# Feed-forward of the first block: inner columns from X times the norm's weights, three side by side, scaled by the tokens' inverse roots on the way out of PSUM

## The chip, the cores and the metric

The kernel runs on one NeuronCore of a Trainium2 chip. TensorE (PE) multiplies, its weight loads (PEld) run beside its matmuls; VectorE (DVE), ScalarE (ACT) and GpSimd (POOL) do the elementwise work, SyncE (SP) starts the weight transfers. Each engine works through its own instructions strictly in the order in which they were written, and waits on semaphores that the others raise. The metric is the device time of one execution in microseconds (us), lower is better: the kernel before has a median of 4513.54 us over three runs (4511.9 to 4514.31).

## The reference

Two blocks follow each other, each with two layers. The change is in the first block only, in both of its layers. Of a layer this matters (S = 512 tokens, D = 1024, FFN = 2816):

```python
def rmsnorm(x, g):
    y = x * rsqrt(mean(x * x, axis=-1) + NORM_EPS)
    return y * g

x = x + rmsnorm(mixed @ w_out, norm_mix_post)
h = rmsnorm(x, norm_ffn_pre)
u = causal_dwconv(h @ w_up, conv_w, conv_b)     # three taps along the tokens, per channel
ua, ub = split(u, (FFN_DIM, FFN_DIM))
x = x + rmsnorm((gelu(ua) * ub) @ w_down, norm_ffn_post)
```

The inverse root of a token is one number for the token's whole row of `h`. It can be multiplied in before the product with `w_up` or behind it. The convolution mixes neighbouring tokens, so it has to come after the multiplication.

## The kernel before, in words

Activations are kept transposed: 128 channels on the partitions, the 512 tokens along the row. X is eight such tiles (DT = 8). A product's output is made in columns: one column is 128 output channels x 512 tokens in one PSUM bank, and takes 8 steps (one per input tile q). Each step is three matmuls (`column_step`, L350, L351, L353), since both operands are split into an upper and a lower part: upper weights x upper input, upper weights x lower input, lower weights x upper input.

Weights come in pieces of 8 tiles (512 KB), one per column here, into a ring of four slots. SP starts the transfers in the order of a fixed list, and waits before each until its slot is free (`weights`, L334). A "cut" piece is split in two: ACT writes the upper part (`act_cuts`, L297, `whi`), DVE then the lower part (`dve_cuts`, L307, `wlo`). There are two buffers of each, so ACT can cut piece k only when PE has done with piece k-2. A "raw" piece goes to PE uncut; its slot is free when PE has used it. In the feed-forward stage the list is: two cut pieces (two columns of `w_up`), two raw pieces, two cut, two raw, and so on, 22 times. The raw pieces are for sums that the second block needs (`modulation_sums`, L1913); PE makes them behind each odd column (`pe_tick`). In this text the cut pieces of the stage are numbered 0, 1, 2, ...; column n uses piece n.

`dense` writes the order of each engine: for each column first the cuts that come due, then the column's own work (the `_tick` functions). Ahead of the columns stands `first_norms`: it makes the sum of squares of the last product Z (`stat_sum`, `stat_root`, `stat_inverse`, `stat_spread`: PE, ACT, DVE, PE), adds the normed Z to X tile by tile (`add_normed`: DVE L518 and L521 for even tiles, POOL L529 for odd ones), then makes the squares of X (ACT L369), their sum, root, inverse and spread again, and only then `norm_to`: h (DVE L475), its upper part (ACT L451), its lower part (DVE L461). Columns 0 and 1 are made interleaved, as the tiles of h come (`two_columns`). In the stage, ACT copies each column out of PSUM into a buffer `u` (L1990), DVE does the three taps (L2003, L2006, L2009), ACT the gelu (L1993), POOL the product of the two halves (L2022), ACT and DVE the upper and lower part of that (L1964, L1968).

Of the kernel before, what the change touches and what calls it, by code (L numbers as in the profile page):

```python
# [7 lines left out]
F32 = mybir.dt.float32  # L8
# [6 lines left out]
P = 128  # L15
D = 1024
DT = D // P
# [83 lines left out]
LAG, PLACES = 4, 8  # L101
GP = 4
# [46 lines left out]
class Prog:  # L149
# [410 lines left out]
    def dense(self, cols, xh, xl, segs, banks_of, free, ready=None, pe_tick=None, act_tick=None,  # L560
              dve_tick=None, pool_tick=None, paired=False, hold=None):
# [4 lines left out]
        def pe():  # L566
            for n, steps in enumerate(cols):
                if paired and n == 0:
                    self.two_columns(cols, xh, xl, segs, banks_of, ready)
                elif not (paired and n == 1):  # L570
                    free(n)
                    self.column(steps, xh, xl, segs, banks_of(n), ready if n == 0 else None)
# [14 lines left out]
        def dve():  # L587
            self.dve_cuts(min(first + 1, self.ahead(first)))
            for n, steps in enumerate(cols):
                for st in steps:  # L590
                    if st.at + st.n == PIECE:
                        self.dve_cuts(self.ahead(st.cut) if hold is None else min(hold, self.ahead(st.cut)))
                if dve_tick:
                    dve_tick(n, steps[-1].value)
# [9 lines left out]
    def columns(self, n_out, kt, paired=False):  # L604

        steps = self.plan(n_out * kt)
        cols = [steps[n * kt:(n + 1) * kt] for n in range(n_out)]
        if paired:
# [10 lines left out]
    def hybrid_sems(self):  # L619
# [26 lines left out]
        self.s_emb = sem("embedded")  # L646

    def hybrid(self, layer, added):
# [49 lines left out]
        b_lo = self.recurrence_out(layer)  # L698
        return self.layer_embedding(layer, *self.conv_ffn(layer, b_lo))
# [1185 lines left out]
    def first_norms(self, Z, b_z, st, cut):  # L1885

        V, A, G = self.V, self.A, self.G
        V.wait_ge(self.s_z.h, b_z + DT)
        G.wait_ge(self.s_ld_x.h, self.s_ld_x.n)
        V.wait_ge(self.s_ld_x.h, self.s_ld_x.n)  # L1890
# [3 lines left out]
        self.x_added(V, b_add, DT - 1)  # L1894
        return self.norm_to(self.view("h", 6144, DT, S), SEG1, lambda j, si: self.p1("fpre", j), (4, 5, 6, 7),
                            Stats(self, A1 + 24000, S, 6), h_hi, h_lo, ready=lambda j: self.x_added(A, b_add, j))
# [40 lines left out]
    def conv_ffn(self, layer, b_lo):  # L1937
# [9 lines left out]
        ub = [self.view(f"u{i}", TF + i * 520, 520) for i in range(4)]  # L1947
        cv = [self.view(f"cv{i}", TF + 2080 + i * S, S) for i in range(4)]
# [9 lines left out]
        cols = self.columns(2 * FT, DT, True)  # L1958
# [21 lines left out]
        def act_tick(n, value):  # L1980
# [16 lines left out]
        def dve_tick(n, value):  # L1997
            q, h = divmod(n, 2)
            i, at = 2 * (q % 2) + h, q + FT * h
            V.wait_ge(self.s_u.h, b_u + n + 1)  # L2000
# [1203 lines left out]
def layout(i):  # L3204
    f = {n: np.asarray(v) for n, v in i.items()}
    ws = []
    for l in range(L):
# [10 lines left out]
        up, down = _inter(f["w_up"][l][:, :FFN], f["w_up"][l][:, FFN:]), _tiles(f["w_down"][l])  # L3218
        ada = _blocks(f["ada_w_2"][l])
# [92 lines left out]
```

## Time and profile before

| what | value |
|---|---|
| median of 3 runs | 4513.54 us (4511.9 to 4514.31) |
| the profiled execution | 4518.9 us, of which the span of the instructions is 4517.4 us |
| PE busy | 4186.4 us (93%) |
| PEld busy | 3242.8 us (72%) |
| DVE busy | 1965.6 us (44%) |
| ACT busy | 1514.9 us (34%) |
| POOL busy | 570.3 us (13%) |
| first norms and feed-forward of layer 0 | from about 867 us to about 1180 us for the inner columns |
| the same of layer 1 | starts at about 2219 us |
| granted TensorE clock, mean | 0.969 of full speed |

A row of the chain of waits says when a link began, how long it held the end, and which engine and line it was. A row of the timeline says start, duration, engine, line, output <- inputs, and in brackets how long the engine was idle before, and what ended that. A duration on DVE or ACT overlaps the next instruction's start a little, so the distance between two starts is what an instruction costs in a row of them.

### The profile page before, as it was taken

To read this page: it belongs to the slowest core of one execution; us is meant where nothing else is said; L and a number is where in the kernel's file an instruction comes from. 1 tells how busy PE (TensorE), PEld (TensorE's weight loads), DVE (VectorE), ACT (ScalarE), POOL (GpSimd) and SP (SyncE) were. 2 spreads that over 40 slices of the span, in tenths; PEclk is the share of its full clock that TensorE was granted. 3 is DMA by queue.
4 is the path that set the end of the run, shared out by engine and by line. 5 is a ranking of instruction groups with operands and counts; after the bars stand their busy time and mean duration, and the time that the engine had idled before them with its cause. 6 is when DMAs were issued, how large, how long until landed. Compare 5 with 4: busy or idle time off the path is not lost.

```text
span 4517.4 us, 73554 instructions
## 1 busy us (share of the span) xinstructions
PE 4186.4 (93%) x32028; PEld 3242.8 (72%) x32028; DVE 1965.6 (44%) x2957; ACT 1514.9 (34%) x2699; POOL 570.3 (13%) x402
## 2 busy tenths in 40 slices
PE   7999779899997999779899998988899999989999
PEld 5776676677775776776677776755688888667877
DVE  5536434455335536434455334357332231444232
ACT  3533233333333533223333333247221121343221
POOL 1215100011002215100011001012000000150000
PEclk9999999999998999999999998999999999999999
DMA  4132002244323132003244321100111211101222
GB/s 160 38 103 69 33 4 94 70 172 173 141 88 104 39 106 70 31 4 104 80 172 171 136 84 43 52 29 1 36 58 61 66 61 61 56 6 62 97 92 87
DMA packets 97681, 351.69 MB, mean 78 GB/s; under 512 B 10064, under 2 KB 13648, under 8 KB 95952
## 3 DMA queue, kind: packets, MB, share of 16 engines
q1 hardware_dynamic: 86480, 313.02, 20.2%
q10 hardware_dynamic: 10880, 33.96, 2.0%
q8 instruction: 254, 4.16, 0.4%
q14 instruction: 67, 0.55, 0.0%
HBM read 332.26 MB, written 14.68 MB: 77 GB/s over the span
## 4 chain that ended last, share of the span: by engine, by line
PE 82%; DVE 8%; issue 3%; POOL 3%; ACT 3%; ACTq 0%; DMA 0%; DVEq 0%; POOLq 0%; SPq 0%
PE ps L350 20%; PE ps L351 19%; PE ps L353 19%; PE ps L1368 7%; PE ps L2395 1%; PE ps L1913 1%; DVE sml L2470 1%; PE ps L391 1%; POOL e L2929 1%; PE ps L2842 1%; DVE x L521 1%; POOL dd L1218 1%; POOL ops L1234 1%; PE ps L888 1%; POOL ops L1226 1%
## 5 line engine op out<-in xcount | busy, mean ns | idle before, releaser
L307 DVE TENSOR_TENSOR wlo<-ring,whi 128x1024 fp32r<-128x1024 f32 x494 | 623.7, 1263 | 1828.6 <-ACT whi L297 1828.2
L297 ACT CAST whi<-ring 128x1024 fp32r<-128x1024 f32 x494 | 517.4, 1048 | 2094.4 <-PE ps L353 1822.6
L350 PE MATMUL ps<-h_hi,whi 128*128 128x512 f32 x1424 | 595.8, 418 | 17.7 <-DVE h_lo L461 10.2
L351 PE MATMUL ps<-h_lo,whi 128*128 128x512 f32 x1424 | 570.7, 401 | 0.0
L353 PE MATMUL ps<-h_hi,wlo 128*128 128x512 f32 x1424 | 569.9, 400 | 0.0
L350 PE MATMUL ps<-hm_hi,whi 128*128 128x512 f32 (+1 forms) x1408 | 514.3, 365 | 16.0 <-DVE hm_lo L464 14.4
L351 PE MATMUL ps<-hm_lo,whi 128*128 128x512 f32 (+1 forms) x1408 | 480.7, 357 | 0.0
L353 PE MATMUL ps<-hm_hi,wlo 128*128 128x512 f32 (+1 forms) x1408 | 418.9, 355 | 0.0
L350 PEld LDWEIGHTS ps<-h_hi,whi 128*128 128x128 f32 x1424 | 273.7, 192 | 160.3 <-issue 62.2
L350 PE MATMUL ps<-ac_hi,whi 128*128 128x512 f32 x880 | 330.3, 375 | 3.0 <-DVE wlo L307 3.0
L350 PEld LDWEIGHTS ps<-hm_hi,whi 128*128 128x128 f32 x1408 | 267.1, 190 | 86.0 <-DVE hm_lo L464 19.6
L351 PEld LDWEIGHTS ps<-h_lo,whi 128*128 128x128 f32 x1424 | 273.7, 192 | 66.5 <-issue 8.2
L353 PEld LDWEIGHTS ps<-h_hi,wlo 128*128 128x128 f32 x1424 | 273.5, 192 | 65.4
L351 PE MATMUL ps<-ac_lo,whi 128*128 128x512 f32 x880 | 318.9, 371 | 0.0
L351 PEld LDWEIGHTS ps<-hm_lo,whi 128*128 128x128 f32 x1408 | 267.1, 190 | 47.2 <-issue 4.8
L353 PE MATMUL ps<-ac_hi,wlo 128*128 128x512 f32 x880 | 297.4, 370 | 0.0
L353 PEld LDWEIGHTS ps<-hm_hi,wlo 128*128 128x128 f32 x1408 | 229.7, 189 | 19.2
L350 PEld LDWEIGHTS ps<-ac_hi,whi 128*128 128x128 f32 x880 | 165.5, 188 | 48.5 <-issue 11.7
L351 PEld LDWEIGHTS ps<-ac_lo,whi 128*128 128x128 f32 x880 | 165.7, 188 | 30.8
L353 PEld LDWEIGHTS ps<-ac_hi,wlo 128*128 128x128 f32 x880 | 152.3, 188 | 23.7
L1368 PE MATMUL ps<-zz 64*64 64x64 f32 (+1 forms) x2560 | 123.2, 239 | 10.8 <-ACT zz L1547 4.0
L2022 POOL TENSOR_TENSOR ac<-cv,cv 128x512 f32<-128x512 f32 x44 | 68.9, 1567 | 503.8 <-DVE cv L2009 503.8
(387 smaller groups left out, 7214.5 us busy)
## 6 DMA issues: line engine op xcount, KB each, us to landing
ring<-in_w SPq DMA_DIRECT2D x590, 512.0 KB, 3.3
h_spill<-h ACTq DMA_DIRECT2D x2, 2048.0 KB, 6.7
x_spill<-x ACTq DMA_DIRECT2D x2, 2048.0 KB, 14.7
m_spill<-m ACTq DMA_DIRECT2D x2, 2048.0 KB, 9.9
h_again<-h_spill ACTq DMA_DIRECT2D x2, 2048.0 KB, 9.0
ma<-m_spill ACTq DMA_DIRECT2D x2, 2048.0 KB, 10.2
x<-x_spill ACTq DMA_DIRECT2D x2, 2048.0 KB, 9.8
x<-in_x SPq DMA_DIRECT2D x4, 512.0 KB, 7.6
```

The source lines that it names most:

```text
L297: self.A.copy(self.hi[k % 2][:], raw).then_inc(self.s_cut_hi.h, 1)
L307: self.V.tensor_tensor(self.lo[k % 2][:], raw, self.hi[k % 2][:].bitcast(F32), ALU.subtract).then_inc(self.s_cut_lo.h, 1)
L350: T.matmul(ps[:, b, 0:cw], hi, xh(q, c0, cw), start=q == 0, stop=False, skip_group_check=True)
L351: T.matmul(ps[:, b, 0:cw], hi, xl(q, c0, cw), start=False, stop=False, skip_group_check=True)
L353: m = T.matmul(ps[:, b, 0:cw], lo, xh(q, c0, cw), start=False, stop=last, skip_group_check=True)
L391: m = T.matmul(self.ps[32 * g:32 * g + 32, st.bank, 0:w], self.c("ones_d", 32), st.sq[j % 2][:, g * w:(g + 1) * w], start=j == 0, stop=j = ...
L521: V.tensor_tensor(self.X[:, j, 0:S], self.X[:, j, 0:S], Z[:, j, :], ALU.add).then_inc(self.s_xadv.h, 1)
L888: T.matmul(ps[:, 7, :], hi, hh(q, 0, S), start=q == 0, stop=False, skip_group_check=True)
L1218: G.tensor_tensor(dd[n % 2][:], zb[n % 2][:, 0:S], zb[n % 2][:, 1:S + 1], ALU.subtract).then_inc(self.s_dd.h, 1)
L1226: self.gq(G.tensor_tensor(BB[:, j, :], kn[i][:], BB[:, j, :], ALU.mult))
L1368: i = T.matmul(ps[dst, 4 * g + bank, at + j * wide:at + (j + 1) * wide], lt(src, GP * g + j), rh(src, GP * g + j), start=begin and j == 0 ...
L2022: G.tensor_tensor(AC[:, q, :], cv[i][:], cv[i - 1][:], ALU.mult).then_inc(self.s_glu.h, 1)
```

## The change

`first_norms` now makes the upper and lower part of X times the norm's weights `fpre` right behind each added tile of X, with no inverse root in it. All adds are on DVE, none on POOL. `columns` and `dense` take `side=3`: columns 0, 1 and 2 are made side by side, 9 matmuls for each tile of the input, and behind each tile the sum of its squares. The weights of those three columns are laid out so that a piece holds them in that order. The inverse roots are spread into PSUM bank 3 in the middle of column 3, copied to SBUF once (`root`), and each column is then taken out of PSUM by a DVE multiplication with `root` in place of the ACT copy. For that the DVE tick stands ahead of the DVE cuts (`tick_first`). The cuts of pieces 2, 3 and 4 are now written inside `first_norms`.

```diff
+    def side_columns(self, cols, xh, xl, segs, banks_of, ready, beside):
+        for q in range(len(cols[0])):
+            ready(q)
+            for c, steps in enumerate(cols):
+                self.column_step(steps, q, xh, xl, segs, banks_of(c))
+            beside(q)
...
     def first_norms(self, Z, b_z, st, cut):
-        b_add = self.add_normed(Z, lambda j: self.p1("post", j), st, [DT - 1], (2, 3, 4, 5), cut=cut)
...
-        return self.norm_to(self.view("h", 6144, DT, S), SEG1, lambda j, si: self.p1("fpre", j), (4, 5, 6, 7),
-                            Stats(self, A1 + 24000, S, 6), h_hi, h_lo, ready=lambda j: self.x_added(A, b_add, j))
+        late = {4: first + 2, 7: first + 3}
...
+            for j in range(DT):
+                A.wait_ge(self.s_xadv.h, b_add + j + 1)
+                A.activation(h_hi[:, j, :], self.X[:, j, 0:S], ACT.Identity,
+                             scale=self.p1("fpre", j)).then_inc(self.s_nhi.h, 1)
+                self.stat_square(st2, j, self.X[:, j, 0:S])
+                if j in late:
+                    self.act_cuts(late[j])
+            self.stat_root(st2)
+            self.act_cuts(first + 4)
...
+        def lower(j):
+            V.wait_ge(self.s_nhi.h, b_hi + j + 1)
+            V.scalar_tensor_tensor(h_lo[:, j, :], self.X[:, j, 0:S], self.p1("fpre", j), h_hi[:, j, :].bitcast(F32),
+                                   ALU.mult, ALU.subtract).then_inc(self.s_nlo.h, 1)
...
+            for j in range(DT):
+                z = self.by_bank(banks, Z[:, j, :])
+                V.scalar_tensor_tensor(z, z, self.p1("post", j), self.spread_of(banks, 0, S), ALU.mult,
+                                       ALU.mult).then_inc(self.s_zn.h, 1)
+                if j >= 1:
+                    lower(j - 1)
+                V.wait_ge(self.s_zn.h, b_zn + j + 1)
+                V.tensor_tensor(self.X[:, j, 0:S], self.X[:, j, 0:S], Z[:, j, :], ALU.add).then_inc(self.s_xadv.h, 1)
+                if j in late:
+                    self.dve_cuts(late[j])
+            lower(DT - 1)
+            self.stat_inverse(st2)
+            self.dve_cuts(first + 4)
...
         def act_tick(n, value):
...
             if n == 0:
-                A.wait_ge(self.s_vq.h, zeroed)
-            A.wait_ge(self.s_mm.h, value)
-            if q >= 2:
-                A.wait_ge(self.s_conv.h, b_conv + n - 3)
-            A.copy(ub[i][:, 2:S + 2], ps[:, n % 4, :]).then_inc(self.s_u.h, 1)
+                A.wait_ge(self.s_rsq.h, st2.spread + 1)
+                A.copy(root[:], ps[:, 3, :]).then_inc(self.s_rootc.h, 1)
...
         def dve_tick(n, value):
+            if n == 0:
+                V.wait_ge(self.s_vq.h, zeroed)
+                V.wait_ge(self.s_rootc.h, b_root + 1)
+            V.wait_ge(self.s_mm.h, value)
+            if q >= 2:
+                V.wait_ge(self.s_conv.h, b_conv + n - 3)
+            V.tensor_tensor(ub[i][:, 2:S + 2], ps[:, bank(n), :], root[:], ALU.mult).then_inc(self.s_u.h, 1)
+            if h == 1 and 0 <= q - 3 < early:
+                lower(q - 3)
```

Three places show how the instructions move. Each row is the line in its own kernel, the operation and its operands, and in brackets the semaphores that it waits for.

First DVE, from the add of the normed Z on. Before, `z` is Z, `x` is X, and the rows end where h begins:

```order
L307 TENSOR_TENSOR wlo0<-ring,whi0 128x1024 [waits cut_hi]
L518 SCALAR_TENSOR_TENSOR z_8290<-z_8290,par,ps 128x512 [waits rsq]
L518 SCALAR_TENSOR_TENSOR z_8290<-z_8290,par,ps 128x512
L521 TENSOR_TENSOR x_49<-x_49,z_8290 128x512 [waits z_normed]
L518 SCALAR_TENSOR_TENSOR z_8290<-z_8290,par,ps 128x512 x2
L521 TENSOR_TENSOR x_49<-x_49,z_8290 128x512 [waits z_normed]
```

The same place on DVE in the changed kernel, at the fifth and sixth tile (`h3_lo` is the lower part of the columns' input, `wlo1` here is piece 2):

```order
L1945 SCALAR_TENSOR_TENSOR z_8290<-z_8290,par,ps 128x512
L1934 SCALAR_TENSOR_TENSOR h3_lo_9446<-x_49,par,h3_hi_9445 128x512 [waits n_hi]
L1950 TENSOR_TENSOR x_49<-x_49,z_8290 128x512 [waits z_normed]
L308 TENSOR_TENSOR wlo1<-ring,whi1 128x1024 [waits cut_hi]
L1945 SCALAR_TENSOR_TENSOR z_8290<-z_8290,par,ps 128x512
L1934 SCALAR_TENSOR_TENSOR h3_lo_9446<-x_49,par,h3_hi_9445 128x512 [waits n_hi]
```

Each tile now has three DVE instructions instead of the two and a half of adding and norming apart, and the cut of piece 2 stands in the middle of them; the cut of piece 3 stands in the same way behind the last add and ahead of the last lower part.

Second ACT, from the root of X's squares to the first gelu. Before (`inv` is the root, `h3_hi` the upper part of h, `whi1` and `whi0` are pieces 2 and 3):

```order
L378 ACTIVATE inv<-ps,con 128x128 [waits sq_mm]
L451 CAST h3_hi_9492<-h_95 128x512 [waits normed] x8
L1955 DMA pe_in_9622<-in_p 128x1024
L297 CAST whi1<-ring 128x1024 [waits mm,w_full3]
L1990 COPY u0_9614<-ps 128x512 [waits mm,dve_seq]
L297 CAST whi0<-ring 128x1024 [waits mm,w_full0]
L1990 COPY u1_9615<-ps 128x512 [waits mm]
L1993 ACT_TABLE_LOAD
L1993 ACTIVATE cv0_9618<-cv0_9618 128x512 [waits conv]
```

The same place on ACT in the changed kernel (`whi0` is piece 3, `whi1` piece 4, `h3_inv` is `root`, the last `whi0` piece 5):

```order
L378 ACTIVATE n_sq34240_512_1_9448<-x_49 128x512 [waits sq_mm]
L298 CAST whi0<-ring 128x1024 [waits mm,w_full0]
L387 ACTIVATE inv<-ps,con 128x128 [waits sq_mm]
L298 CAST whi1<-ring 128x1024 [waits mm,w_full3]
L2018 DMA pe_in_9574<-in_p 128x1024
L2051 COPY h3_inv_9569<-ps 128x512 [waits rsq]
L2054 ACT_TABLE_LOAD
L2054 ACTIVATE cv0_9570<-cv0_9570 128x512 [waits conv]
L298 CAST whi0<-ring 128x1024 [waits mm,w_full0]
```

The copies to `u` are gone, and the copy of the inverse roots stands behind the cut of piece 4, which waits for that piece's transfer (`w_full3`).

Third DVE, at the first columns. Before (`wlo0`, `wlo1`, `wlo0` are pieces 3, 4 and 5):

```order
L307 TENSOR_TENSOR wlo0<-ring,whi0 128x1024 [waits cut_hi]
L2003 TENSOR_SCALAR cv1_9619<-u1_9615,par 128x512 [waits u_copied]
L2006 SCALAR_TENSOR_TENSOR cv1_9619<-u1_9615,par,cv1_9619 128x512 [waits dve_seq]
L2009 SCALAR_TENSOR_TENSOR cv1_9619<-u1_9615,par,cv1_9619 128x512 [waits dve_seq]
L307 TENSOR_TENSOR wlo1<-ring,whi1 128x1024 [waits cut_hi]
L2003 TENSOR_SCALAR cv2_9620<-u2_9616,par 128x512 [waits u_copied]
L2006 SCALAR_TENSOR_TENSOR cv2_9620<-u2_9616,par,cv2_9620 128x512 [waits dve_seq]
L2009 SCALAR_TENSOR_TENSOR cv2_9620<-u2_9616,par,cv2_9620 128x512 [waits dve_seq]
L307 TENSOR_TENSOR wlo0<-ring,whi0 128x1024 [waits cut_hi]
```

The same place on DVE in the changed kernel. Ahead of these rows stand the cut of piece 4, column 0's four instructions and column 1's `u`; the last row is the cut of piece 5:

```order
L2073 TENSOR_SCALAR cv1_9571<-u1_9566,par 128x512 [waits u_copied]
L2076 SCALAR_TENSOR_TENSOR cv1_9571<-u1_9566,par,cv1_9571 128x512 [waits dve_seq]
L2079 SCALAR_TENSOR_TENSOR cv1_9571<-u1_9566,par,cv1_9571 128x512 [waits dve_seq]
L2067 TENSOR_TENSOR u2_9567<-ps,h3_inv_9569 128x512 [waits mm]
L2073 TENSOR_SCALAR cv2_9572<-u2_9567,par 128x512 [waits u_copied]
L2076 SCALAR_TENSOR_TENSOR cv2_9572<-u2_9567,par,cv2_9572 128x512 [waits dve_seq]
L2079 SCALAR_TENSOR_TENSOR cv2_9572<-u2_9567,par,cv2_9572 128x512 [waits dve_seq]
L2067 TENSOR_TENSOR u3_9568<-ps,h3_inv_9569 128x512 [waits mm]
L2073 TENSOR_SCALAR cv3_9573<-u3_9568,par 128x512 [waits u_copied]
L2076 SCALAR_TENSOR_TENSOR cv3_9573<-u3_9568,par,cv3_9573 128x512 [waits dve_seq]
L2079 SCALAR_TENSOR_TENSOR cv3_9573<-u3_9568,par,cv3_9573 128x512 [waits dve_seq]
L308 TENSOR_TENSOR wlo0<-ring,whi0 128x1024 [waits cut_hi]
```

Between the cuts of pieces 4 and 5 DVE had one column's three instructions before; now it has four columns' sixteen.

## Rows read from the trace of the kernel before

**Rows 1.** The page's part 4: the chain that ended last, by engine.

```profile
PE 82%; DVE 8%; issue 3%; POOL 3%; ACT 3%; ACTq 0%; DMA 0%; DVEq 0%; POOLq 0%; SPq 0%
```

**Rows 2.** The chain of waits in layer 0's first norms: start, us, engine, line.

```profile
869.67 1.11 DVE wlo L307
870.77 1.33 DVE z L518 x2
872.12 1.26 DVE x L521
...
881.78 1.22 PE ps L391 x16
...
886.81 0.70 DVE h_lo L461
887.55 0.79 PE ps L350
888.35 0.43 PE ps L351
```

**Rows 3.** Busy time by stretch, layer 0: PE, PEld, DVE, ACT, POOL, granted clock, DMA.

```profile
872.00:873.00 1.00, 0.00 (x0) 0.00 (x0) 0.97 (x2) 0.00 (x0) 0.84 (x1) 0.76 0.74 299
...
893.00:894.00 1.00, 1.00 (x6) 0.83 (x5) 1.00 (x3) 0.62 (x1) 0.00 (x0) 1.00 0.00 0
```

**Rows 4.** Timeline of POOL, the first odd tile's add.

```profile
871.58 1.26 POOL L529 TENSOR_TENSOR x<-x,z 128x512 f32<-128x512 f32 x1 [102.43 <-DVE z L518]
```

**Rows 5.** DVE's column multiplication out of PSUM, by tile `gb`: ns min/median/max.

```profile
L1854 DVE TENSOR_TENSOR gb<-ps,gb x16: 682/684/685, 780.9 to 2172.7; 128x512 f32<-128x512 f32 x16
```

**Rows 6.** Timeline of ACT: two squares of X, one upper part of h.

```profile
873.42 1.15 ACT L369 ACTIVATE n_sq<-x 128x512 f32<-128x512 f32 x2 [3.90 <-DVE x L521]
...
888.19 0.62 ACT L451 CAST h_hi<-h 128x512 fp32r<-128x512 f32 x1 [0.76 <-DVE h L475]
```

**Rows 7.** Timeline of PE: a sum of squares between matmuls, then raw pieces, then columns.

```profile
860.50 0.39 PE L353 MATMUL ps<-mix_hi,wlo 128*128 128x512 f32 x1
...
861.18 0.50 PE L350 MATMUL ps<-mix_hi,whi 128*128 128x512 f32 x1
...
901.30 1.06 PE L1913 MATMUL ps<-ring,cond 128*32 128x512 f32 x8
902.45 0.51 PE L350 MATMUL ps<-h_hi,whi 128*128 128x512 f32 x1
...
926.97 0.50 PE L350 MATMUL ps<-h_hi,whi 128*128 128x512 f32 x1
```

**Rows 8.** Timeline of DVE: one column's taps between two cuts.

```profile
902.32 0.54 DVE L2003 TENSOR_SCALAR cv<-u,par 128x512 f32<-128x512 f32 x1
902.89 0.75 DVE L2006 SCALAR_TENSOR_TENSOR cv<-u,par,cv 128x512 f32<-128x512 f32 x1
903.68 0.75 DVE L2009 SCALAR_TENSOR_TENSOR cv<-u,par,cv 128x512 f32<-128x512 f32 x1
904.35 1.22 DVE L307 TENSOR_TENSOR wlo<-ring,whi 128x1024 fp32r<-128x1024 f32 x1
905.49 0.54 DVE L2003 TENSOR_SCALAR cv<-u,par 128x512 f32<-128x512 f32 x1
```

**Rows 9.** Timeline of ACT: cuts that waited for a transfer, layer 0.

```profile
909.36 1.05 ACT L297 CAST whi<-ring 128x1024 fp32r<-128x1024 f32 x1 [4.26 <-DMA ring<-in_w]
...
921.08 1.05 ACT L297 CAST whi<-ring 128x1024 fp32r<-128x1024 f32 x1 [5.13 <-DMA ring<-in_w]
```

**Rows 10.** Timeline of SP's queue: the fourth transfer behind the first raw pieces.

```profile
905.59 0.33 SPq L334 DMA_DIRECT2D ring<-in_w  x1
```

**Rows 11.** Timeline of PE in the second block: a column behind a short gap.

```profile
4400.74 0.47 PE L350 MATMUL ps<-ac_hi,whi 128*128 128x512 f32 x1 [2.12 <-DVE wlo L307]
```

**Rows 12.** Busy time by stretch behind that gap, columns as in rows 3.

```profile
4402.00:4405.00 3.00, 3.00 (x8) 2.30 (x7) 0.00 (x0) 0.00 (x0) 0.00 (x0) 0.50 0.83 274
```

More of the change, by code:

```diff
@@ L560, in dense @@
     def dense(self, cols, xh, xl, segs, banks_of, free, ready=None, pe_tick=None, act_tick=None,
-              dve_tick=None, pool_tick=None, paired=False, hold=None):
+              dve_tick=None, pool_tick=None, paired=False, hold=None, side=0, beside=None, between=None,
+              tick_first=False):
         first = cols[0][0].cut
@@ L569, in pe @@
                     self.two_columns(cols, xh, xl, segs, banks_of, ready)
-                elif not (paired and n == 1):
+                elif side and n == 0:
+                    self.side_columns(cols[:side], xh, xl, segs, banks_of, ready, beside)
+                elif not (paired and n == 1) and n >= side:
                     free(n)
-                    self.column(steps, xh, xl, segs, banks_of(n), ready if n == 0 else None)
+                    self.column(steps, xh, xl, segs, banks_of(n), ready if n == 0 else between(n) if between else None)
                 if pe_tick:
@@ L589, in dve @@
             for n, steps in enumerate(cols):
+                if tick_first:
+                    dve_tick(n, steps[-1].value)
                 for st in steps:
@@ L592, in dve @@
                         self.dve_cuts(self.ahead(st.cut) if hold is None else min(hold, self.ahead(st.cut)))
-                if dve_tick:
+                if dve_tick and not tick_first:
                     dve_tick(n, steps[-1].value)
@@ L602, in dense, with columns @@
         return pe(), act(), dve(), pool()
-    def columns(self, n_out, kt, paired=False):
+    def columns(self, n_out, kt, paired=False, side=0):
         steps = self.plan(n_out * kt)
         cols = [steps[n * kt:(n + 1) * kt] for n in range(n_out)]
+        for c in range(side):
+            cols[c] = steps[c:side * kt:side]
         if paired:
@@ L1895, in first_norms @@
-        return self.norm_to(self.view("h", 6144, DT, S), SEG1, lambda j, si: self.p1("fpre", j), (4, 5, 6, 7),
-                            Stats(self, A1 + 24000, S, 6), h_hi, h_lo, ready=lambda j: self.x_added(A, b_add, j))
+        st2 = Stats(self, A1 + 24000, S, 6)
+        b_zn, b_add = self.s_zn.take(DT), self.s_xadv.take(DT)
+        b_hi, b_lo = self.s_nhi.take(DT), self.s_nlo.take(DT)
+        cols, banks = self.columns(2 * FT, DT, side=SIDE), (2, 3, 4, 5)
+        first = cols[0][0].cut
@@ new lines, in first_norms, with pe, act @@
+        late = {4: first + 2, 7: first + 3}
+        def pe():
+            self.stat_sum(st, DT - 1)
+            self.stat_spread(st, banks)
+            yield
+        def act():
+            self.stat_root(st)
+            self.act_cuts(cut)
+            for j in range(DT):
[7 more added lines that the diff above has]
+            self.act_cuts(first + 4)
+            yield
@@ L1935, in modulation_sums, with conv_ffn @@
         return pe, pe_back, act, dve
[L1937 removed]
+    def conv_ffn(self, layer, cols, b_lo, st2):
         T, V, A, G, ps = self.T, self.V, self.A, self.G, self.ps
@@ L1947, in conv_ffn @@
         ub = [self.view(f"u{i}", TF + i * 520, 520) for i in range(4)]
+        root = self.view("h3_inv", A1 + FT * S, S)
         cv = [self.view(f"cv{i}", TF + 2080 + i * S, S) for i in range(4)]
@@ L1957, in conv_ffn @@
         mod_pe, mod_back, mod_act, mod_dve = self.modulation_sums(layer)
-        cols = self.columns(2 * FT, DT, True)
+        b_root = self.s_rootc.take(1)
+        bank = lambda n: (0, 1, 7, 2)[n % 4]
         b_u, b_conv, b_gelu, b_glu = self.s_u.take(2 * FT), self.s_conv.take(2 * FT), self.s_gelu.take(FT), self.s_glu.take(FT)
```

31 lines of the change are left out of this document (19 added, 12 removed).

## Prediction

> **What bounds the kernel now.** I read the page's chain first: four fifths of it are PE [rows 1], so a change pays only where PE stands still, and costs wherever it makes PE stand still. Then the chain in order of time through layer 0's first norms [rows 2]. From 867 us to 887.55 PE makes nothing but sums of squares and spreads; the end hangs on DVE's pairs of norm and add (L518, L521), a last sum, a root, an inverse and the first tile of h. From 902.45 to 926.97 the timeline shows no idle time on PE: four columns and two sets of raw pieces in 24.52 us [rows 7]. A set costs 902.45 - 901.30 = 1.15 us, 1.24 with its entry, so a column is (24.52 - 2.48) / 4 = 5.51 us and a matmul 0.23. What I look for is how much earlier PE can start, and what then falls due earlier than DVE, ACT and the transfers can give it.
>
> All steps are put on layer 0's clock. Up to 870.77 us, where DVE begins with the normed Z, nothing changes.
>
> **The start.** Z's first tile takes DVE 0.74 us (half of an x2 row of 1.33 and its tail) [rows 2]. Its add took 1.26 us, from 872.12 to 873.38, while POOL was busy with its own add until 871.58 + 1.26 = 872.84 [rows 2, 4]. With POOL gone I take what a DVE tensor_tensor costs elsewhere, 0.68 [rows 5], 0.70 for h_lo [rows 2]; the upper bound is 1.26. The Trainium skill, SBUF — State Buffer, Who interferes with whom, says that a DVE instruction with two SBUF inputs is fully blocked by a GpSimd instruction that reads SBUF and started first. The rows agree, since DVE's add ended 0.54 us behind POOL's; without that rule eight adds would stay at 1.26, and DVE would be 8 x 0.58 = 4.6 us later by the last tile. Then ACT's upper part 0.62 [rows 6], DVE's lower part 0.75 (a tap has the same form, two SBUF inputs and a scalar) [rows 8]: 870.77 + 0.74 + 0.68 + 0.62 + 0.75 and 0.15 of semaphores is 873.7. PE starts at 873.75 instead of 887.55, **13.8 us earlier**. From there DVE gives a tile every 0.66 + 0.66 + 0.62 + 0.05 = 2.0 us.
>
> **Three columns side by side.** Per tile PE has 9 x 0.23 = 2.07 us of matmuls and a sum of squares. Such a sum costs 861.18 - 860.50 - 0.23 = 0.45 us, and the matmul behind it 0.05 more [rows 7]: 2.57 us a tile, 20.6 for eight. These sums lay in the idle stretch before; now they are 4 us of the stream. The granted clock had fallen to its lower level (1.2 GHz) during 872 to 873 (mean 0.76) and was at the upper one again at 893, 5.4 us behind the first dense matmul [rows 2, 3]; at half speed that costs 2.7 us, before and after alike. So PE would be done at 873.75 + 20.6 + 2.7 = 897.0 if it never waited. It waits twice. ACT may make a square only when the sum two tiles back is done. PE ends the sums of tiles 2 and 3 at about 884.0 and 886.6; so ACT squares tile 4 until 884.5 (0.58, half of 1.15 [rows 6]) and cuts piece 2 until 885.6 [rows 9]; DVE, which stands at this cut with Z's tile 5 and the lower part of tile 4 behind it, ends it at 886.8 and these two at 888.2. PE is idle for 1.6 us. At tile 7 the same order (square, cut of piece 3, lower part) gives 897.2 where PE is ready at 896.1: 1.1 us. The side columns end at **899.8**, with 897.0 and 901.5 (one more fall of the clock, below) as bounds, and the raw set behind them at 901.0. Before, it was at 902.45 with one column fewer: the lead is 1.4 + 5.5 = 7 us here.
>
> **Behind it: piece 4 and four columns in a row on DVE.** This step decides. SP starts the raw pieces' successors when PE has used them, and piece 4 stands behind these two in SP's list. Before, ACT could cut piece 4 at 909.36, 6.9 us behind the end of the raw set (902.45); in the next pair 921.08 - 914.71 = 6.4 us [rows 7, 9]. Nobody missed it: two columns lay between. Now only column 3 and a raw set do. I take 6.9: 907.9. ACT cuts until 909.0 and then copies the roots; DVE cuts until 910.2 (a cut costs it 905.49 - 904.35 = 1.14 [rows 8]). DVE's columns 0 to 3 all stand behind this cut in its queue, and piece 5 behind them. A column is now u out of PSUM (0.68 [rows 5] and 0.09 until the tap sees it) and three taps, 904.35 - 902.32 = 2.03 [rows 8]: 2.8 us, four of them 11.2, until 921.4. Piece 5's cut ends at 922.6, and **column 5 starts at 922.7**. Between 901.0 and 922.7 PE has columns 3 and 4, a raw set and a spread, some 13 us of work, in 21.7: it first waits for column 0's bank, which u frees, until about 911, and stands still from about 916.5 to 922.7. Column 5 and its raw set end at 922.7 + 5.51 + 1.24 = 929.4, against 926.97 before: **2.4 us later**. The lead of 13.8 is gone: 4 in the sums of squares, 2.7 in the two waits, about 1 in the spread, 8 in these two gaps.
>
> **The clock.** Behind an idle stretch of 2.12 us PE was at the lower level 1.3 us later, for at least 3 us [rows 11, 12], a price of 1.5 to 1.7 us. A gap of 6.2 us ahead of column 5 should cost as much at least, 2.7 at most (the first start above), nothing at best. I take 1.7: **4.1 us later** per layer.
>
> **From there on** PE is the bound again. DVE has per column 2.8 us and a cut of 1.14, in odd columns 0.68 more, of 5.51 to 6.75: cut n+2 ends 4.0 to 4.8 us behind column n and is wanted 6.7 behind it. ACT's 44 copies a layer go, under PE, and are worth nothing. Their cover for DVE's new work is the 2 us left; if DVE were 2 us slower per column, each column would pay. No SP transfer waits longer: a cut that is 2 us later frees a slot that is read 12 us on. Nothing behind the feed-forward gives time back or takes any.
>
> **Sum.** Two layers with the same code: 2 x 4.1 = +8.2 us. On the profiled execution's own time, 4518.9 (span 4517.4), that is 4527.1; the median of the runs is 5.4 below it, so I forecast 4513.5 + 8.2 = **4521.7 us**. The case's own range is 4518 to 4525. About 0.2% (9 us) is what a measurement of this kernel can tell from no change, so this counts as the same, close to the edge.
>
> **Rivals.**
> 1. *The wait for piece 5 doesn't bind, and the lead is kept.* Behind 901.0 come three columns, two raw sets and a spread of about 1: 921.0, 6 us ahead of 926.97; two layers give 4501.5. For it speaks that DVE is busy for only 44% of the span. Against it the order: piece 5's cut would have to be 8 us earlier, and it stands behind sixteen instructions that stand behind a transfer which can't start before PE has used the raw pieces. A misread dependence is what would bring it.
> 2. *The clock falls more often.* The gaps of 1.6 and 1.1 us in the side columns are shorter than the 2.12 us of rows 11, but PE has light sums beside them. One fall there shifts the whole chain by 1.7, and the restart of column 5 may cost 2.7: +6.8 a layer, 4527.1. It decides from the point at which a gap under 2 us is enough.
> 3. *Piece 4 comes earlier.* The fourth transfer was issued at 905.59 [rows 10] and shares the 6.9 us. If they land in order, piece 4 needs about three quarters of it, 5.2 to 5.7: 1.5 us less a layer, 4518.7. The Trainium skill, DMA: Bandwidth & Descriptors, Queues, rings and completion order, says that each DMA engine consumes descriptors in ring order but that completion is not first in, first out; by its first half this rival holds, by its second the 6.9 may stay. The trace leaves it open.
>
> **How the numbers follow.** The forecast 0.45, rival 1 0.15, rival 2 0.25, rival 3 0.15. Faster than by 0.2% is most of rival 1: 0.13. Slower (over 4522.6) is nearly all of rival 2 and two fifths of the forecast: 0.43. The rest, 0.44, is the same. The range leaves out rival 1 and what goes beyond rival 2: 4508 to 4529.
>
> **What would show it.** In the profile after: PE's first column matmul about 14 us earlier in each layer; two short gaps in the side columns, released by DVE's lower part; ACT's cut of piece 4 released by a transfer; four `u` and their taps on DVE without a pause, ahead of a `wlo`; PE idle for about 6 us ahead of column 5, released by DVE's `wlo`, and the clock at half behind it. If that last gap is missing or under 2 us, the forecast is wrong and rival 1 right. If the raw set of columns 4 and 5 ends before 927 on layer 0's clock, the sign is wrong.

## The result, and the profile after

The changed kernel takes 4522.49 us (median of 13 runs, 4515.50 to 4529.54) where the kernel before, run beside it, takes 4513.54 (13 runs, 4503.49 to 4521.72). The ratio is 1.0022, with a 95% interval of 1.0014 to 1.0031: 9.9 us slower, 6 to 14 by the interval. The prediction was 4521.7.

The two profiled executions say nothing of this by themselves: 4518.9 us before and 4518.85 after. Outside the stretches that the change touches, where both run the same code, the one of after happened to be 8.5 us shorter: 3.0 ahead of layer 0's first norms, 4.1 between the two stretches, 1.4 behind them. The nine changed kernels of this document scatter there by 8.4 us (3664.7 to 3673.2 us, where before's trace has 3677.4). So the two are compared over each stretch by itself, from one event on: the first norm of Z in a layer, DVE's first `z`. The first two rows are before's, from DVE's and PE's timelines: that norm, and the sum of squares that PE makes when layer 0's feed-forward is over.

```profile
870.69 1.40 DVE L518 SCALAR_TENSOR_TENSOR z<-z,par,ps 128x512 f32<-128x512 f32 x2
```

```profile
1290.74 0.43 PE L391 MATMUL ps<-n_sq,con 128*32 128x128 f32 x8 [0.33 <-ACT n_sq L369]
```

The same two in the profile after:

```profile
867.72 0.74 DVE L1945 SCALAR_TENSOR_TENSOR z<-z,par,ps 128x512 f32<-128x512 f32 x1
```

```profile
1292.12 0.43 PE L400 MATMUL ps<-n_sq,con 128*32 128x128 f32 x8 [0.33 <-ACT n_sq L378]
```

The distance is 420.05 us before and 424.40 after: 4.35 longer. In layer 1 it is 2642.56 - 2222.64 = 419.92 and 2643.84 - 2219.88 = 423.96: 4.04 longer. Together 8.4 us, inside the interval of the ratio. I call this distance the *stage*; it is the measure for the experiments too. It comes from one trace of each kernel.

The page's part 4 after, which answers to [rows 1]:

```profile
PE 81%; DVE 8%; issue 4%; POOL 3%; ACT 3%; DMA 0%; ACTq 0%; DVEq 0%; SPq 0%; POOLq 0%
```

One point has gone from PE to "issue", which tells nothing of where. The chain of waits in layer 0 does (start, us, engine, line; it answers to [rows 2]; add 2.96, which is 870.77 - 867.81, for before's clock):

```profile
867.81 0.67 DVE z L1945
868.50 0.70 DVE x L1950
869.23 0.73 ACT h_hi L1923
869.98 0.76 DVE h_lo L1934
870.79 0.79 PE ps L351
...
881.59 1.04 ACT whi L298
882.65 1.23 DVE wlo L308
...
896.98 0.98 PE ps L1975 x8
898.26 0.43 SPq L335
898.74 6.34 DMA ring<-in_w
905.10 1.05 ACT whi L298
906.17 0.50 DVE wlo L308
...
907.53 0.70 DVE u L2067
...
919.03 1.23 DVE wlo L308
920.39 0.76 PE ps L351
```

To be read: PE's columns begin 2.98 us behind the first norm, against 887.55 - 870.77 = 16.78 before, so 13.8 of lead. Then, from 898.26 to 920.39, the chain leaves PE for 22 us: it goes over SP, a transfer, ACT's and DVE's cut, four columns on DVE and the next cut. Before, PE held the chain through this stretch [rows 7].

PE's timeline shows the same from the other side. The bracket is the idle time before the row and what ended it; the rows with L1975 are the raw sets:

```profile
885.25 0.51 PE L351 MATMUL ps<-h_hi,whi 128*128 128x512 f32 x1 [1.63 <-DVE h_lo L1934]
...
894.28 0.51 PE L351 MATMUL ps<-h_hi,whi 128*128 128x512 f32 x1 [1.06 <-DVE h_lo L1934]
...
896.80 1.04 PE L1975 MATMUL ps<-ring,cond 128*32 128x512 f32 x8
897.77 0.50 PE L351 MATMUL ps<-h_hi,whi 128*128 128x512 f32 x1
...
904.39 1.07 PE L1975 MATMUL ps<-ring,cond 128*32 128x512 f32 x8
...
908.28 0.50 PE L351 MATMUL ps<-h_hi,whi 128*128 128x512 f32 x1 [2.82 <-DVE u L2067]
...
920.39 0.76 PE L351 MATMUL ps<-h_hi,whi 128*128 128x512 f32 x1 [6.32 <-DVE wlo L308]
...
928.58 0.51 PE L351 MATMUL ps<-h_hi,whi 128*128 128x512 f32 x1
```

These are all four waits that the prediction named. The first two are the cuts of pieces 2 and 3 between DVE's tiles, the third is column 4 waiting for column 0's bank, the fourth is column 5 waiting for piece 5. The lead of 13.8 us is used up, and column 5 with its raw set ends at 928.58 + 2.96 = 931.54 on before's clock, where it was 926.97 [rows 7]: 4.6 us late. In layer 1 the last two idles are 2.66 and 4.76, with the clock down behind the first as well. That second fall costs nothing: column 5 starts 2272.20 - 2260.07 = 12.13 us behind column 4 there and 920.39 - 908.28 = 12.11 in layer 0, since DVE's cut sets its start, and the slower column 4 only shortens the idle time behind it.

The account of layer 0: the four waits are 1.63 + 1.06 + 2.82 + 6.32 = 11.8 us. Eight sums of squares come on top: a tile takes PE 2.63 us, of which 9 x 0.23 are the columns' matmuls, so 4.5 in all. The spread in column 3 takes 904.39 - 897.77 - 5.51 = 1.1, and the clock behind the last gap 1.4. These 18.8 us stand against the 13.8 won and the 4.6 lost, which make 18.4: the account closes to 0.4 us.

DVE's timeline from the cut of piece 4 to that of piece 5 (answers to [rows 8]; the cut of piece 4 on ACT, in the chain above at 905.10, answers to [rows 9]):

```profile
906.17 1.23 DVE L308 TENSOR_TENSOR wlo<-ring,whi 128x1024 fp32r<-128x1024 f32 x1 [7.77 <-ACT whi L298]
...
907.53 0.69 DVE L2067 TENSOR_TENSOR u<-ps,h_inv 128x512 f32<-128x512 f32 x1
...
910.29 0.68 DVE L2067 TENSOR_TENSOR u<-ps,h_inv 128x512 f32<-128x512 f32 x1
...
913.77 1.01 DVE L2073 TENSOR_SCALAR cv<-u,par 128x512 f32<-128x512 f32 x1
...
919.03 1.22 DVE L308 TENSOR_TENSOR wlo<-ring,whi 128x1024 fp32r<-128x1024 f32 x1
```

DVE stands for 7.77 us and then works without a pause, 2.76 us a column, up to the cut of piece 5. One tap of the sixteen instructions takes 1.01 instead of 0.55.

Three stretches: the first cold phase, the one behind it, and the second (columns as in [rows 3]; the granted clock is the third number from the end):

```profile
870.00:872.00 2.00, 1.21 (x3) 1.02 (x4) 1.99 (x3) 1.10 (x3) 0.00 (x0) 0.50 0.25 102
...
876.00:878.00 2.00, 2.00 (x13) 1.36 (x15) 1.36 (x3) 0.89 (x2) 0.00 (x0) 1.00 0.04 8
...
918.00:920.00 2.00, 0.00 (x0) 0.00 (x0) 1.96 (x3) 0.00 (x0) 0.81 (x1) 0.50 0.00 0
920.00:922.00 2.00, 1.61 (x4) 1.35 (x5) 1.93 (x4) 0.00 (x0) 1.38 (x1) 0.50 0.34 98
```

Column 5 runs its first 3 us at 1.2 GHz. Column and raw set take 928.58 - 920.39 = 8.19 us instead of 5.51 + 1.24.

### The profile page after: what moved, and what is told of

Read it like the earlier page. It is cut to its first block, busy times and chain, and to the rows that moved or that the text cites. A ratio compares the mean times of both kernels' runs of the same rounds, so it can differ in the third digit from the quotient of the medians.

```text
span 4517.3 us, 73524 instructions
## 1 busy us (share of the span) xinstructions
PE 4178.5 (92%) x32028; PEld 3233.9 (72%) x32028; DVE 2015.4 (45%) x3037; ACT 1473.6 (33%) x2613; POOL 586.8 (13%) x394
## 4 chain that ended last, share of the span: by engine, by line
PE 81%; DVE 8%; issue 4%; POOL 3%; ACT 3%; DMA 0%; ACTq 0%; DVEq 0%; SPq 0%; POOLq 0%
PE ps L351 20%; PE ps L352 19%; PE ps L354 19%; PE ps L1383 7%; PE ps L2467 1%; PE ps L1975 1%; DVE sml L2542 1%; PE ps L400 1%; POOL e L3001 1%; DVE wlo L308 1%; PE ps L2914 1%; POOL ops L1249 1%; POOL dd L1233 1%; POOL ops L1241 1%; ACT whi L298 1%
## 5 line engine op out<-in xcount | busy, mean ns | idle before, releaser
L354 PEld LDWEIGHTS ps<-hm_hi,wlo 128*128 128x128 f32 x1408 | 229.5, 189 | 19.3
L2090 POOL TENSOR_TENSOR ac<-cv,cv 128x512 f32<-128x512 f32 x44 | 95.3, 2167 | 707.0 <-DVE cv L2079 707.0
## 6 DMA issues: line engine op xcount, KB each, us to landing
x_spill<-x ACTq DMA_DIRECT2D x2, 2048.0 KB, 13.9
```

The source lines that it names most:

```text
L354: m = T.matmul(ps[:, b, 0:cw], lo, xh(q, c0, cw), start=False, stop=last, skip_group_check=True)
```

## The experiments

The theory: the change gives PE 13.8 us. The sums of squares and the spread cost 5.6 of them in every kernel below; two things take back the rest and more. Behind the side columns there is one column left to cover the transfer of piece 4 and DVE's queue behind it (the cut of piece 4, columns 0 to 3, the cut of piece 5); and the third side column makes DVE's stream of tiles slower than PE by two cuts. The rivals: the extra work on PE and the clock (rival A in the expectations), or a DVE that is too full in the whole stage, so that any gain is taken back behind the gaps (rival B).

All kernels below start from the changed one. This table holds, per kernel, the stage less before's in layers 0 and 1 (from each one's trace), their sum, and the ratio to before with its interval, in us of 4513.5. The ratio on record is not that of the two medians: for e4 the medians are 13.9 us apart (4496.87 beside 4510.79), for e6 18.0.

| kernel | stage, layer 0 | layer 1 | sum | ratio to before (95%) | in us |
|---|---|---|---|---|---|
| after | +4.35 | +4.04 | +8.4 | 1.0022 (1.0014 to 1.0031) | +9.9 |
| e1_raw_early | -0.1 | +0.9 | +0.7 | 1.0003 (0.9994 to 1.0012) | +1.4 |
| e2_cut_between | -1.5 | -1.5 | -3.0 | 1.0001 (0.9992 to 1.0010) | +0.5 |
| e3_both | -4.6 | -4.6 | -9.2 | 0.9986 (0.9977 to 0.9995) | -6.3 |
| e4_two_side | -8.4 | -8.2 | -16.6 | 0.9964 (0.9951 to 0.9976) | -16.2 |
| e5_fill | +2.9 | +2.6 | +5.5 | 1.0015 (1.0007 to 1.0024) | +6.8 |
| e6_two_side_cut4 | -9.6 | -9.7 | -19.3 | 0.9965 (0.9952 to 0.9977) | -15.8 |
| e7_two_side_warm | -10.2 | -10.1 | -20.3 | 0.9963 (0.9951 to 0.9976) | -16.7 |
| e8_both_warm | -6.5 | -4.2 | -10.7 | 0.9978 (0.9969 to 0.9987) | -9.9 |

Every sum lies inside the interval of its ratio. So these two stretches hold the whole difference within what the ratios can tell, and nothing behind them gives or takes more than the intervals' 4 to 6 us.

**The first raw set earlier (e1).** PE makes the first raw set behind the sum of tile 6 and not behind the last side column. SP's transfers start earlier by that.

```diff
-            if n % 2:
+            if n % 2 and n > 1:
                 mod_pe(n // 2)
...
+        def beside(q):
+            self.stat_sum(st2, q)
+            if q == 6:
+                T.wait_ge(self.s_zn.h, z_read)
+                mod_pe(0)
```

> The changed kernel with the first raw set made behind the sum of squares of tile 6 in the side columns, where PE stood idle for 1.06 us, instead of behind the side columns. Nothing else is moved. Theory (the lead is lost in one chain: raw set, transfer of piece 4, its cuts, four columns on DVE, cut of piece 5): the raw set ends about 3.5 us earlier, so ACT's cut of piece 4, the four columns and the start of column 5 all come 3.5 us earlier, the gap of 6.3 us ahead of column 5 stays as long as it is: about -3.5 us a layer against the changed kernel, -7 in all, so about +2 against the kernel before (4513.5 to 4518). Rival A (the extra PE work and the clock take the lead, the transfer is only seen in the trace): only the 1.06 us of idle time is used, -1 a layer, -2 in all, about +7 against before. Rival B (DVE is too full in the whole stage because it now takes the columns out of PSUM): no change, +9.

Measured 1.0003 (0.9994 to 1.0012): 4513.81 us against 4510.79 for before beside it, and 8 us better than the changed kernel. ACT's timeline, then PE's:

```profile
897.55 1.05 ACT L298 CAST whi<-ring 128x1024 fp32r<-128x1024 f32 x1 [2.96 <-DMA ring<-in_w]
```

```profile
912.85 0.77 PE L351 MATMUL ps<-h_hi,whi 128*128 128x512 f32 x1 [5.35 <-DVE wlo L308]
```

Piece 4 is cut 897.55 - 865.11 = 32.4 us behind the first norm, 4.9 earlier than after's 905.10 - 867.72 = 37.4 (3.5 were expected; the raw set ends 4.0 earlier and the transfer takes 6.3 us and not 7.3), and column 5 starts 47.7 behind it, not 52.7. The gap ahead of column 4 is gone: column 0 is out of its bank in time. The long gap stays at 5.35, since all of DVE's queue moved with piece 4. The transfer is what starts DVE's queue, one for one.

**The cuts of pieces 4 and 5 behind column 0 (e2).** DVE does column 0 while the transfers are still under way.

```diff
             self.stat_root(st2)
-            self.act_cuts(first + 4)
...
             self.stat_inverse(st2)
-            self.dve_cuts(first + 4)
...
                 A.copy(root[:], ps[:, 3, :]).then_inc(self.s_rootc.h, 1)
+                self.act_cuts(cols[0][0].cut + 5)
...
+            if n == 0:
+                self.dve_cuts(cols[0][0].cut + 5)
```

> The changed kernel with the cuts of pieces 4 and 5 moved, on ACT behind the copy of the inverse roots, on DVE behind column 0 (before: piece 4 ahead of column 0, piece 5 behind column 3). Theory: column 0 is done while piece 4 is still under way; the cuts of 4 and 5 end about 1.2 and 2.4 us behind ACT's first (907.3 and 908.5 on the clock of the changed kernel's trace, layer 0), so columns 4 and 5 run on without a gap, column 5's raw set ends at about 919.7 instead of 928.7: -9 us a layer, -18 in all, about -9 against before (4504.5, ratio 0.998). Rival A (extra PE work and the clock): the clock price of 2 us a layer goes with the gap and the rest stays: -4 in all, +5 against before. Rival B (DVE too full): the work is only moved, the gap comes back ahead of column 6 or 7: within 2 us of the changed kernel.

Measured 1.0001 (0.9992 to 1.0010). This misses the expectation: of the 18 us against the changed kernel 9.5 came by the ratio and 11.4 by the stages. DVE's timeline, then PE's:

```profile
906.74 2.45 DVE L308 TENSOR_TENSOR wlo<-ring,whi 128x1024 fp32r<-128x1024 f32 x2 [1.96 <-ACT whi L298]
```

```profile
908.11 0.47 PE L351 MATMUL ps<-h_hi,whi 128*128 128x512 f32 x1 [2.65 <-DVE wlo L308]
...
920.92 1.06 PE L1973 MATMUL ps<-ring,cond 128*32 128x512 f32 x8
...
922.43 0.47 PE L351 MATMUL ps<-h_hi,whi 128*128 128x512 f32 x1 [0.45 <-DVE wlo L308]
```

The long gap ahead of column 5 is gone. But column 4 needs piece 4, and that is no earlier: PE waits 2.65 us for it. Columns 4 and 5 with the raw set then take 921.98 - 908.11 = 13.9 us where 2 x 5.51 + 1.24 = 12.3 would do, since the clock fell behind this gap (0.50 from 910 to 912). The loss has two causes, the transfer and DVE's order, and taking away the second alone leaves PE waiting for the first.

**Both (e3).**

> Both moves together: the first raw set behind the sum of tile 6, and the cuts of pieces 4 and 5 behind column 0 on DVE. By the traces of the two alone, column 6 starts (behind column 5 and its raw set) 56.5 us after Z's first norm with the early raw set, 54.9 with the moved cuts, 60.8 in the changed kernel, 56.2 in the kernel before. Theory (one chain, whose links are the transfer and DVE's row of columns): piece 4 has landed when column 0 is done, the gap ahead of column 4 shrinks from 2.65 to under 0.5 us, the fall of the clock behind it goes, and what is left is piece 6, which stands behind DVE's columns 1 to 4: column 6 at about 51.5, -4.7 a layer against before, -9.4 in all (ratio 0.998). Rival (each move only shifts the same loss; DVE's four columns bind whatever is done): no better than the moved cuts alone, ratio 1.000.

Measured 0.9986 (0.9977 to 0.9995), by the stages -9.2 us. In PE's timeline the gap ahead of column 4 is 1.08 (under 0.5 was expected), with no fall of the clock behind it, and one of 1.95 stands ahead of column 6, whose piece DVE now cuts last. Column 6 starts 919.49 - 867.58 = 51.9 us behind the first norm (51.5 expected):

```profile
905.23 0.47 PE L351 MATMUL ps<-h_hi,whi 128*128 128x512 f32 x1 [1.08 <-DVE wlo L308]
...
919.49 0.47 PE L351 MATMUL ps<-h_hi,whi 128*128 128x512 f32 x1 [1.95 <-DVE wlo L308]
```

The stages give -9.2 as expected, and the interval holds that value, but its middle is 3 us short of it. Three columns side by side can thus beat the kernel before. The change from loss to gain lies in the order behind them; the multiplication at PSUM is in this kernel too and takes nothing back later in the stage (rival B).

**Two columns side by side (e4).** Two columns beside the norms instead of three; no cut stands between DVE's tiles any more. The cut of piece 4 moves as well, from ahead of column 0 to behind column 2 in DVE's order (the expectation names only columns 0 and 1 ahead of it).

```diff
-SIDE = 3
+SIDE = 2
...
-        late = {4: first + 2, 7: first + 3}
+        late = {}
...
+            self.act_cuts(first + 2)
             self.stat_root(st2)
-            self.act_cuts(first + 4)
+            self.act_cuts(first + 3)
...
             lower(DT - 1)
+            self.dve_cuts(first + 2)
             self.stat_inverse(st2)
-            self.dve_cuts(first + 4)
+            self.dve_cuts(first + 3)
```

> The changed kernel with two columns side by side instead of three; the cut of piece 2 behind the last lower part and of piece 3 behind the inverse, no cut between the tiles, piece 4 left to the columns' own order (column 0 and 1 stand ahead of it on DVE). Theory: PE starts as early as with three; the side columns are 48 matmuls and 8 sums with a cold start, 11.0 + 4.0 + 2.7, done about 18 us behind their start and not stopped by cuts; the raw set ends 9 us ahead of the kernel before (which had made the same two columns by then), the spread gives back 1, and piece 4 has two columns to come in: about -7.5 us a layer against before, -15 in all (4498.5, ratio 0.9967). Rival A (extra PE work and the clock): the sums and the clock are there too, and a third column less lies under DVE's chain, so PE waits for DVE's tiles (2.14 us each) instead: 0 to -3 against before. Rival B (DVE too full in the stage): +5 or more against before as in the changed kernel.

Measured 0.9964 (0.9951 to 0.9976): 4496.87 us, -16.2, and -16.6 by the stages. PE's timeline:

```profile
878.04 0.43 PE L400 MATMUL ps<-n_sq,con 128*32 128x128 f32 x8
...
879.98 0.43 PE L400 MATMUL ps<-n_sq,con 128*32 128x128 f32 x8
...
887.99 1.04 PE L1977 MATMUL ps<-ring,cond 128*32 128x512 f32 x8
...
903.72 0.47 PE L351 MATMUL ps<-h_hi,whi 128*128 128x512 f32 x1 [1.55 <-DVE wlo L308]
```

A tile is 1.94 us on PE with no wait, the raw set comes 20.2 us behind the first norm and not 29.1, and piece 4's transfer is covered by columns 2 and 3. One gap of 1.55 us is left, behind which the clock did not fall. The loss of 9.9 is a gain of 16. This run changes three things at once (the number of columns, the cuts between the tiles, DVE's place for piece 4), so by itself it does not say which gave how much, and no run keeps three columns and takes only the cuts out from between the tiles. PE's idle times say it: in layer 0, from the first column to column 6, they are 11.8 us in the changed kernel, 4.9 in e3, 1.55 here and none in e6 below. The stages are 14.0, 5.0 and 1.2 us longer than e6's: the waits, and in the changed kernel the clock's 1.4 beside them, are the difference. The two between the tiles, 2.7 us in the changed kernel, are gone here.

**The gap filled (e5).** Five fp32 matmuls whose result nobody reads stand behind column 4. This tells the price of the clock from the price of the wait.

```diff
+            if n == 4:
+                T.wait_ge(self.s_rootc.h, b_root + 1)
+                for _ in range(5):
+                    T.matmul(ps[:, 3, :], self.c("ident"), self.X[:, 0, 0:S], start=True, stop=True,
+                             skip_group_check=True)
```

> The changed kernel with five plain fp32 matmuls (128x128 by 128x512, into the free bank 3, read by nobody) behind column 4, in the gap of 6.3 us ahead of column 5; they take about 0.86 us each. It measures the price of the clock's fall alone. Theory: PE's clock stays at its upper level through the gap, column 5 runs at full speed from its first matmul: -2 us a layer, -4 in all against the changed kernel, about +5 against before; the start of column 5 (DVE's cut of piece 5) doesn't move. Rival A (the clock is most of the loss): -4.5 a layer, about 0 against before. Rival B (DVE too full): as the theory, since it says nothing on the clock.

Measured 1.0015 (1.0007 to 1.0024), +6.8 us; against the changed kernel -2.9 by the stages, where -4 was expected. PE's timeline, then the stretch in which column 5 starts (clock third from the end):

```profile
912.39 4.45 PE L2046 MATMUL ps<-x,con 128*128 128x512 f32 x10
...
917.32 0.47 PE L351 MATMUL ps<-h_hi,whi 128*128 128x512 f32 x1 [0.47 <-DVE wlo L308]
...
923.02 1.07 PE L1975 MATMUL ps<-ring,cond 128*32 128x512 f32 x8
```

```profile
916.00:918.00 2.00, 1.53 (x5) 0.64 (x5) 1.96 (x4) 0.00 (x0) 1.88 (x1) 1.00 0.00 0
```

Column 5 starts as late as in the changed kernel, 52.75 us behind the first norm against 52.67, but at the full clock: its matmuls take 923.02 - 917.32 = 5.70 us, against 927.58 - 920.39 = 7.19. The clock's price is 1.5 us a layer here (1.4 and 1.5 by the stages). The waits and the extra work of PE cost the rest. So the clock as the main cause is refuted: it makes a third of the 9. (In this kernel the clock fell behind the gap ahead of column 4, 3.02 us in layer 0 and 2.79 in layer 1; this lies ahead of the filled gap and does not move column 5's start.)

**Two side columns, piece 4's cut behind column 1 (e6).** On e4, DVE's cut of piece 4 stands two columns earlier, to take the gap of 1.55 away.

```diff
+            if n == 1:
+                self.dve_cuts(cols[0][0].cut + 4)
```

> Two columns side by side as in the run before, with DVE's cut of piece 4 behind column 1 instead of behind column 2. There DVE's cut ended at 903.6 (2.36 us late) and PE stood idle for 1.55 us ahead of column 4. Theory: the piece has landed at 897.7, so the cut is done 2.8 us earlier and the gap goes: column 6 starts 46.6 us after Z's first norm instead of 48.2, -1.6 a layer, so -19 in all against before (ratio 0.9958). Rival (DVE is behind anyway): the gap moves ahead of column 5, ratio stays at 0.9964.

Measured 0.9965 (0.9952 to 0.9977), 4491.39 us beside 4509.35. The gap is gone, and column 6 starts 47.0 us behind the first norm (46.6 expected): in layer 0 PE's timeline has no idle time from the first column to the raw set of columns 4 and 5, and the stages are 2.7 us shorter in sum than e4's. The ratio can't tell it from e4's 0.9964, since five runs give an interval of 11 us; so this gain is seen in the traces alone.

**PE kept at work before its first column (e7, e8).** Three fp32 matmuls without use stand behind the spread of Z's norm, on e6 and on e3.

```diff
+            for _ in range(3):
+                T.matmul(ps[:, 0, :], self.c("ident"), self.con[:, 0:S], start=True, stop=True, skip_group_check=True)
```

> The same with three plain fp32 matmuls (into bank 0, overwritten by column 0) between the spread of Z's inverse roots and the first column, where PE stood idle for 3.5 us; each takes 0.89 us. They keep PE busy ahead of the cold start. Theory that the side columns are bound by DVE, which gives a tile every 2.14 us and the last at 885.9, with PE done at 888.2: the clock stays up, but only 0.3 to 0.8 us a layer come of it (ratio 0.9955 to 0.9958). Rival (the cold start costs PE its 2.3 to 2.7 us in full): -2.5 a layer against the kernel without them, ratio 0.9947.

> Three columns side by side, both moves, and the same three matmuls ahead of the first column. Here PE and not DVE is behind in the first tiles (the squares wait for PE's sums, the cut of piece 2 for the square of tile 4), so the theory says that the cold start counts in full: everything from the cut of piece 2 on comes 2.3 us earlier, column 6 about 49.2 us after Z's first norm, -7 a layer against before, -14 in all (ratio 0.9969). Rival (DVE binds the side columns here as well): no more than with both moves alone, ratio 0.998.

Measured 0.9963 (0.9951 to 0.9976) for e7 and 0.9978 (0.9969 to 0.9987) for e8. In e8's trace PE begins at the full clock, which its first matmul shows (0.50 us, not 0.79):

```profile
866.12 2.84 PE L1917 MATMUL ps<-con 128*128 128x512 f32 x6
869.72 0.50 PE L351 MATMUL ps<-h_hi,whi 128*128 128x512 f32 x1 [0.76 <-DVE h_lo L1935]
...
889.75 1.04 PE L1975 MATMUL ps<-ring,cond 128*32 128x512 f32 x8
```

With three side columns PE is what paces the first tiles, and the raw set comes 1.9 us earlier behind the first norm in layer 0 (23.09 against e3's 25.00) and 1.2 in layer 1. With two, DVE paces them and the gain is 0.6 and 0.4 us. Neither ratio is apart from that of the kernel without these matmuls, so these gains are seen in the traces alone. By the stages e8 keeps its gain in layer 0 and loses it again in layer 1, where the stage is 0.4 us longer than e3's; the sum is -10.7 where -14 was expected, and the ratio that of the rival. In layer 0 the -6.5 is close to the theory's -7. The stretches behind the gap ahead of column 6 tell what differs: the gap is 1.96 us in layer 0 and 1.95 in layer 1, and only in layer 1 did the clock fall behind it.

```profile
918.00:920.00 2.00, 2.00 (x11) 1.62 (x10) 1.96 (x3) 0.00 (x0) 0.65 (x1) 1.00 0.94 356
...
2262.00:2264.00 2.00, 2.00 (x6) 1.52 (x6) 1.87 (x2) 0.00 (x0) 1.18 (x1) 0.50 0.71 270
```

## Why the prediction was right

All on layer 0's clock, after's times with 2.96 added, the prediction's in brackets.

- **Start of the columns:** 873.75 (873.75). Norm 0.67, add 0.70, upper part 0.73, lower part 0.76. The sizes of the parts were off by up to 0.1 and cancelled: ACT's upper part now comes straight from X with a scale for each partition and takes 0.73, not the 0.62 of the plain copy [rows 6]. POOL's removal did bring the add from 1.26 to 0.70, as the step on the shared read took it.
- **Pace of the tiles:** DVE's and ACT's loop took 871.37 - 869.23 = 2.14 us (2.0). It cost nothing, since PE needs 2.63 a tile (2.57). Counted with the lower part, DVE had three and a half instructions a tile before and has three now.
- **The two short waits:** 1.63 and 1.06 (1.6 and 1.1); side columns and raw set at 900.73 (901.0).
- **Piece 4:** ACT cuts at 908.06 (907.9). From the end of the raw set that is 7.33 us, against 6.91 before and 5.2 to 5.7 for rival 3, which is therefore wrong; e1 has 6.3.
- **DVE's queue:** `u` of column 0 to the cut of piece 5 took 919.03 - 907.53 = 11.50 us (11.2), of it 0.46 for the one tap beside POOL's product, which the prediction did not have.
- **Column 5:** starts at 923.35 (922.7), behind a gap of 6.32 (6.2). The gap ahead of column 4 is 2.82; the prediction gives no size for it alone, but 8 us for the two gaps together, and they are 9.1.
- **The clock behind it:** 8.19 - 6.75 = 1.4 us (1.7), 1.5 by e5.
- **Sum:** 4.6 us by this stretch and 4.35 by the whole stage in layer 0, 4.04 in layer 1 (4.1 each); 8.4 together (8.2), and 9.9 by the ratio.

The mechanism held in each step. The times on the clock that were off lie under 0.7 us and partly cancel: column 5 starts 0.65 later than forecast, and the clock behind it costs 0.3 less. That the median, 4522.49, lies within 0.8 us of the forecast is partly luck: the interval is 4 us wide to each side. What is 1.5 us between stages and ratio stays unexplained and is well inside the interval.

**The rivals.** Rival 1 (the lead is kept) fell: column 5's `wlo` came 11.5 us behind column 0's `u`, as the queue said. Its price, -12, is what e4 and e6 reach and pass, with the waits taken away. Rival 2 (the clock falls once more) fell for the side columns: at 876:878, and in each wait of 1.63 and 1.06, PE stayed at the upper level. One more fall did come, in layer 1, behind the gap of 2.66 ahead of column 4. The prediction had put layers 0 and 1 as alike; the two gaps differ there (2.66 and 4.76 for 2.82 and 6.32), but that fall lay in time in which PE would have waited for piece 5, and the sums are within 0.3 us. Rival 3 is answered under piece 4.

## What to carry to other kernels

When work is started earlier, follow every queue to the first place where the lead must be repaid: here it was a transfer that had taken 6.4 and 6.9 us before but under two columns, and an engine that was 45% busy but had sixteen instructions between two cuts. How much work is put beside a slow stretch is a size to be tried: what is used up there is missing later as cover. Two columns with the cuts moved gained 0.36%, three lost 0.22%, and three with both moves gained 0.14%. If a ratio is at the limit of what can be told, a distance between two events in the trace, on both sides of the change, tells 1 us where the ratio tells 5.

## What the runs showed of the hardware

- DVE's TENSOR_SCALAR out of and into SBUF is held by POOL's tensor_tensor. POOL's product (913.22, 1.28 us, first row) makes the tap that starts at 913.77 end 0.28 us behind it, at 914.78; under the next one the tap at 920.89 takes 0.77 and ends 0.28 us behind it too. The `u` of 920.17 (one input from PSUM, one from SBUF) takes its usual 0.68 under the same product. The Trainium skill, SBUF — State Buffer, Who interferes with whom, lists tensor_scalar among the operations that can take the port pair that DVE shares with GpSimd; the trace agrees, with 1.01 us for 0.55.

```profile
913.22 1.28 POOL L2090 TENSOR_TENSOR ac<-cv,cv 128x512 f32<-128x512 f32 x1 [147.04 <-DVE cv L2079]
919.19 2.19 POOL L2090 TENSOR_TENSOR ac<-cv,cv 128x512 f32<-128x512 f32 x1 [4.69 <-DVE cv L2079]
```

- The holding goes both ways: POOL's second product starts 0.16 us into DVE's cut of 919.03, which has two inputs in SBUF, and takes 2.19 us for 1.28. Over the whole kernel POOL's 44 products take 2.17 us in the mean where they took 1.57 before. No wait of PE in the rows above is released by POOL.
- Gaps on PE of 1.06, 1.55 and 1.63 us left the clock at its upper level. Behind a gap of 2.65 in e2, of 2.66 in layer 1 of the changed kernel and of 2.79 and 3.02 in e5 it fell, as behind the 2.12 of [rows 11]; behind 2.82 in layer 0 of the changed kernel it did not (the granted clock is 1.00 from 908 to 916). Of four gaps of 1.95 and 1.96, two in e3 and two in e8, only the one in e8's layer 1 was followed by a fall. From 1.95 to 2.82 us the length of the gap alone does not decide. A fall cost 1.4 us in the changed kernel, 1.5 by e5 and 1.6 in e2.
- ACT's activation with a scale for each partition, SBUF to SBUF on 128x512, takes 0.72 us in the changed kernel where the plain copy takes 0.62 before [rows 6].
